# A 1-core transformer block kernel: norm tiles made on VectorE and ScalarE alone, the first two products of a stage run side by side, two waits moved

## What is computed

```python
hl = modulate(rms_norm(xl, norm1_g[i]), mod_l[0], mod_l[1])   # y * (1 + scale) + shift
ol = conv_module(hl, ...)              # block 0: product, gate, 31 taps, layer norm, silu, product
ol, oc = gqa_mixer(hl, hc, ...)        # block 1: qkv product, heads, output product
xl = xl + mod_l[2][:, None, :] * ol
hl = modulate(rms_norm(xl, norm2_g[i]), mod_l[3], mod_l[4])
xl = xl + mod_l[5][:, None, :] * sq_relu_mlp(hl, w_ff1[i], w_ff2[i])
# block 2: rms norm with a gain, an input product, mixers, then experts chosen per token:
# silu(x @ gate) * (x @ up) @ down for each expert slot, gathered and summed
```

## Time and profile before

| | us |
|---|---|
| median of 3 runs | 2501.03 (2499.95 to 2521.93) |
| the profiled execution's own time | 2502.87 |
| its span in the trace | 2501.1 |
| PE busy | 2287.1 |
| DVE busy | 1376.6 |
| ACT busy | 791.2 |
| POOL busy | 733.2 |

### The profile page before, as it was taken

How to read it: one execution, slowest core, us unless ns; L and a number is a source line. 1 busy time by engine, 2 the same in 40 slices (tenths; PEclk the granted TensorE clock), 3 DMA queues, 4 the chain that set the end, 5 groups by cost and what they waited for, 6 DMA issues and landing times.

```text
span 2501.1 us, 30069 instructions
## 1 busy us (share of the span) xinstructions
PE 2287.1 (91%) x11308; PEld 1797.4 (72%) x11308; DVE 1376.6 (55%) x1709; ACT 791.2 (32%) x1068; POOL 733.2 (29%) x409
## 2 busy tenths in 40 slices
PE   6899987899999999897999899999899779799993
PEld 3566746778888888774456688887688667688882
DVE  2488974264444444315663664655222751699994
ACT  2311104221111111331662311211333322577772
POOL 2200001443333333543443544443444034011101
PEclk8899997999999999899999899999899899899996
DMA  8554340162122212130001233333233023499994
GB/s 272 168 167 144 127 165 28 51 252 68 59 67 59 67 59 68 43 91 25 1 1 43 85 93 94 99 92 107 74 93 92 9 71 135 175 397 398 412 397 151
DMA packets 248521, 312.79 MB, mean 125 GB/s; under 512 B 13706, under 2 KB 199787, under 8 KB 236147
## 3 DMA queue, kind: packets, MB, share of 16 engines
q1 hardware_dynamic: 236956, 275.33, 32.6%
q0 software_dynamic: 6688, 25.69, 2.7%
q10 hardware_dynamic: 4791, 10.58, 1.1%
HBM read 286.39 MB, written 25.18 MB: 125 GB/s over the span
## 4 chain that ended last, share of the span: by engine, by line
PE 83%; DVE 8%; DMA 3%; POOL 2%; ACT 2%; issue 2%; DVEq 0%; POOLq 0%; ACTq 0%; SPq 0%
PE acc L494 54%; PE acc L2394 7%; PE pb L2416 4%; PE pb L2046 2%; PE pa L1998 2%; PE acc L2172 2%; DMA mod_raw<-in_w_mod 2%; PE pa L2186 2%; PE pb L2199 2%; PE acc L541 1%; POOL y L620 1%; PE acc L555 1%; DVE hid_hi L1481 1%; PE pa L2384 1%; PE pa L648 1%
## 5 line engine op out<-in xcount | busy, mean ns | idle before, releaser
L477 POOL TENSOR_TENSOR wlo<-raw,whi 128x1024 fp32r<-128x1024 f32 x204 | 509.2, 2496 | 967.3 <-ACT whi L466 967.2
L494 PE MATMUL acc<-ah,whi 128*128 128x256 f32 (+1 forms) x1616 | 514.7, 367 | 57.7 <-DVE al L660 35.7
L466 ACT ACTIVATE whi<-raw 128x1024 fp32r<-128x1024 f32 x218 | 230.4, 1059 | 1054.3 <-PE acc L494 1035.5
L494 PE MATMUL acc<-al,whi 128*128 128x256 f32 (+1 forms) x1616 | 506.9, 363 | 0.0
L494 PE MATMUL acc<-ah,wlo 128*128 128x256 f32 (+1 forms) x1616 | 506.3, 362 | 0.0
L494 PEld LDWEIGHTS acc<-ah,whi 128*128 128x128 f32 x1616 | 307.1, 192 | 119.4 <-issue 42.4
L494 PEld LDWEIGHTS acc<-al,whi 128*128 128x128 f32 x1616 | 310.0, 192 | 47.0 <-issue 0.5
L494 PEld LDWEIGHTS acc<-ah,wlo 128*128 128x128 f32 x1616 | 309.1, 191 | 47.3
L1490 DVE SCALAR_TENSOR_TENSOR x<-acc,mod,x 128x256 f32<-128x256 f32 (+1 forms) x192 | 121.1, 658 | 262.0 <-PE acc L494 261.9
L768 DVE TENSOR_TENSOR expert_lo<-expert_pair,expert_hi 128x1024 fp32r<-128x1024 f32 x192 | 224.4, 1220 | 23.0 <-ACT expert_hi L763 23.0
L494 PE MATMUL acc<-hid_hi,whi 128*128 128x512 f32 (+1 forms) x768 | 230.7, 355 | 0.7 <-DVE x L1490 0.2
(11 more groups left out here) (348 smaller groups left out, 2824.4 us busy)
## 6 DMA issues: line engine op xcount, KB each, us to landing
raw<-in_w_ff SPq DMA_DIRECT2D x128, 512.0 KB, 3.9
mod_raw<-in_w_mod SPq DMA_DIRECT2D x96, 512.0 KB, 5.4
expert_pair<-in_expert_w_gate SPq DMA_DIRECT2D x32, 1024.0 KB, 7.7
expert_pair<-in_expert_w_up SPq DMA_DIRECT2D x32, 1024.0 KB, 7.5
expert_pair<-in_expert_w_down SPq DMA_DIRECT2D x32, 1024.0 KB, 7.2
raw<-in_w_in SPq DMA_DIRECT2D x30, 512.0 KB, 3.9
raw<-in_conv_w_pw SPq DMA_DIRECT2D x24, 512.0 KB, 7.6
expert_rows_dram<-zero_rows POOLq DMA_DIRECT2D x1, 12288.0 KB, 38.4
```

Of the source, the lines that this page charges most:

```text
L466: e.eng.activation(whi[e.n["q"] % 2][:, :], raw[r][:, :], ACT.Copy).then_inc(S["hi_ready"], 1)
L477: e.eng.tensor_tensor(wlo[b][:, :], raw[e.n["g"] % RING][:, :], whi[b][:, :].bitcast(F32), ALU.subtract).then_inc(S["lo_ready"], 1)
L494: ins = e.eng.matmul(o, w, m, start=keys.index(key) == n, stop=len(keys) - 1 - keys[::-1].index(key) == n)
```

## The change

Five edits:

1. A norm tile takes three steps. DVE multiplies x by the root and by the gain or scale in one instruction for each segment, ACT adds the shift and rounds into `ah`, DVE adds the shift and subtracts `ah` into `al`. POOL has no part in it. Tiles run three ahead. The layer norm and the norm with a gain have the same order now.
2. `first_pair`: the first two products behind each of the six norms take turns, tile by tile, in the two PSUM banks. Both need their weights split beforehand, so the second split moves before the tiles on ACT and POOL, and `split_started` is raised one time early in `spread_mean` (in the conv stage by `mod_chunk(18)`), and one time at the last tile of the pair.
3. The first output product behind the attention takes its tiles in the order 0, 1, 2, 3, 4, 6, 5, 7 and waits for `attended` before tile 5.
4. The last expert's down weights go into the buffers 0 to 3.
5. Branches for down pieces that aren't split are dropped (`SPLIT_DOWN` is 4, so they were not used).

```diff
-    def norm_act(e, n, k, segs, k_root, split=True, early=None, affine=None):
+    def norm_act(e, n, k, segs, k_root, early, affine=None):
...
-        if early:
+        early()
+        root(e, k_root, token_stat[:, c0 // P:TOK // P])
+        if n:
             early()
-        root(e, k_root, token_stat[:, c0 // P:TOK // P])
...
         for i in range(KT):
+            e.eng.wait_ge(S["x_scaled"], KT * n + i + 1)
             if affine is None:
...
+                ins = e.eng.activation(ah[:, i, c0:TOK], y[:, i, c0:TOK], ACT.Copy)
             else:
...
-            e.eng.activation(ah[:, i, c0:TOK], y[:, i, c0:TOK], ACT.Copy).then_inc(S["ah_ready"], 1)
-            if k and i == KT - 3:
-                early()
...
+                for s0, s1, v in segs:
+                    at = i + affine[2]
+                    ins = e.eng.activation(ah[:, i, s0:s1], y[:, i, s0:s1], ACT.Identity, bias=mod[:, at:at + 1, v])
+            ins.then_inc(S["ah_ready"], 1)
```

```diff
         def by_root(i):
-            e.eng.tensor_tensor(scaled[i % 3][:, c0:TOK], x[:, i, c0:TOK], token_cols(pa, c0), ALU.mult
-                                ).then_inc(S["x_scaled"], 1)
+            for s0, s1, v in segs:
+                by = cols[:, gain + i:gain + i + 1] if affine is None else msc[:, affine[1], i:i + 1, v]
+                ins = e.eng.scalar_tensor_tensor(out=y[:, i, s0:s1], in0=x[:, i, s0:s1], scalar=by,
+                                                 in1=pa[:, CTX + s0:CTX + s1], op0=ALU.mult, op1=ALU.mult)
+            ins.then_inc(S["x_scaled"], 1)
+
+        def low(i):
+            e.eng.wait_ge(S["ah_ready"], KT * operand + i + 1)
+            for s0, s1, v in segs:
+                hi = ah[:, i, s0:s1].bitcast(F32)
...
+                    ins = e.eng.scalar_tensor_tensor(out=al[:, i, s0:s1], in0=y[:, i, s0:s1], scalar=mod[:, at:at + 1, v],
+                                                     in1=hi, op0=ALU.add, op1=ALU.subtract)
+            ins.then_inc(S["al_ready"], 1)
```

```diff
+    def first_pair(e, segs, operand):
+
+        e.eng.wait_ge(S["lo_ready"], e.at("q", 2))
+        e.eng.wait_ge(S["acc_free"], e.at("u", 2))
+        for t in range(KT):
+            e.eng.wait_ge(S["al_ready"], KT * operand + t + 1)
+            for n in range(2):
+                h, l, bank = whi[(e.n["q"] + n) % 2], wlo[(e.n["q"] + n) % 2], acc[(e.n["u"] + n) % 2]
+                for j, (w, a) in enumerate(((h, ah), (h, al), (l, ah))):
+                    for s0, s1, _ in segs:
+                        ins = e.eng.matmul(bank[:, CTX + s0:CTX + s1], w[:, t * P:t * P + P], a[:, t, s0:s1],
+                                           start=t == 0 and j == 0, stop=t == KT - 1 and j == 2)
+                        if t == KT - 1 and n == 1 and j == 0 and s0 == segs[0][0]:
+                            ins.then_inc(S["split_started"], 1)
+                if t == KT - 1:
+                    ins.then_inc(S["acc_ready"], 1)
+        e.n["u"] += 2
```

```diff
-        load_parts((more, 1), range(8, E_SLOTS, 2))
+        ex = expert_of((more, 1))
+        for s in range(0, 4, 2):
+            sp.wait_ge(S["weights_used"], weights_done((more, 1), s + 1))
+            expert_load(e, ex, s, last=True)
...
-        pe.wait_ge(S["attended"], 1)
-        slots(e, KT, tile(LATENT))
+        pe.wait_ge(S["lo_ready"], e.at("q", 1))
+        pe.wait_ge(S["acc_free"], e.at("u", 1))
+        h, l, bank = whi[e.n["q"] % 2], wlo[e.n["q"] % 2], acc[e.n["u"] % 2]
+        for t in (0, 1, 2, 3, 4, 6, 5, 7):
+            if t == 5:
+                pe.wait_ge(S["attended"], 1)
```

More of the change, by code:

```diff
@@ L478, in split_low, with run_group @@
                             ALU.subtract).then_inc(S["lo_ready"], 1)
-    def run_group(e, group, first=None, last=None, operand=None, per_tile=1):
+    def run_group(e, group, first=None, last=None):
         keys = [g[0] for g in group]
@@ L1390, in _ @@
         e.step(scales(0, 0, 1, V_N1))
-        norm_dve(e, 1, FULL, 1, operand=0, affine=AFFINE[0])
+        norm_dve(e, 0, 1, FULL, 1, 0, AFFINE[0])
         def gated(i):
@@ L1496, in _ @@
         slots(e, KT, to_stream(16, FULL))
-        norm_dve(e, 4, FULL, 3, operand=2, affine=AFFINE[1])
+        norm_dve(e, 1, 4, FULL, 3, 2, AFFINE[1])
         operand_done(e, 3)
@@ L2023, in _, with project, pair @@
         mod_chunk(4, pbk[:, 0:512])
-        def project(i, after=None):
-            product(e, ah, al, FULL, first="split_started" if i % 2 else None, operand=None if i else 0)
+        def project(i):
+            product(e, ah, al, FULL, first="split_started" if i % 2 else None)
             e.n["g"] += 1
             e.n["q"] += 1
+        def pair(segs, operand):
+            first_pair(e, segs, operand)
+            e.n["g"] += 2
+            e.n["q"] += 2
         def turned_at(i, n):
@@ L2106, in down, with up @@
                 product(e, hid_hi[b], hid_lo[b], segs, k=4)
-            feed_forward(e, lambda chunk, j, b: product(
-                e, ah, al, segs, operand=operand if isinstance(chunk, int) and chunk + j == 0 else None), down,
-                beside=beside)
+            def up(chunk, j, b):
+                if isinstance(chunk, int) and chunk == 0 and j < 2:
+                    if j == 0:
+                        first_pair(e, segs, operand)
+                else:
+                    product(e, ah, al, segs)
+            feed_forward(e, up, down, beside=beside)
         spread_mean(e, 1, FULL, 3)
@@ L2122, in sum_heads @@
                           start=n in (0, 1), stop=n in (3, 11)).then_inc(S["qk_summed"], 1)
-        for n in range(12):
+        pair(FULL, 3)
+        sum_heads(0)
+        for n in range(2, 12):
             if n >= 4:
                 pe.wait_ge(S["q_second"], n - 3)
-            product(e, ah, al, LATENT if 2 <= n < 10 else FULL, operand=None if n else 3)
+            product(e, ah, al, LATENT if n < 10 else FULL)
             e.n["g"] += 1
@@ L2253, in used @@
             e.n["q"] += 1
-        for n in range(14):
+        pair(LATENT, 5)
+        for n in range(2, 14):
             if 4 <= n < 8:
@@ L2258, in _ @@
             else:
-                product(e, ah, al, LATENT, operand=None if n else 5)
+                product(e, ah, al, LATENT)
             used()
```

167 lines of the change are left out of this document (60 added, 107 removed).

## The result

| | before | after |
|---|---|---|
| median, us | 2502.35 (4 runs, 2499.95 to 2521.93) | 2476.42 (4 runs, 2473.32 to 2481.44) |
| ratio after / before | | 0.9873, 95% interval 0.984 to 0.9907 |
| span of the profiled execution | 2501.1 | 2474.1 |
| PE busy | 2287.1 | 2284.0 |
| POOL busy | 733.2 | 690.0 |

The forecast was 2468, 32.6 us off the median of before, with a range of 2455 to 2481.

What follows compares the result with a forecast made beforehand. PE, the engine of most of the chain, was taken to lose time waiting, most for `al`, the normed operand's low part. Gains of 39.4 us less 6.8 for clock gave 32.6 off 2501.03: 2468, range 2455 to 2481.

Steps and rivals of the forecast that it cites:

- the forecast case: Whole kernel: all gains arrive, less the clock loss after the third products' waits; 2468, chance 0.62.
- conv: Norm before the conv products: the pair starts without an idle wait and ends at 82.0 instead of 92.1; 10.0 us.
- FF1: Norm before the FF1 products: the third product starts at 519.4 instead of 526.0; 6.6 us.
- head wait: First output product behind the attention: six tiles run first and cover the 3.45 us wait for the last heads; 5.5 us.
- late down weights: Last expert: its down weights load into gate buffers freed earlier, so PE starts at 2453.0, not 2460.39; 7.4 us.
- clock in the third products: After PE's 3 us waits at FF1, conv-out, FF2 and input the clock falls: 1.7 us each, 6.8 lost.
- The tiles: Norm tiles: DVE sets the pace, a pair of instructions every 1.05 us, a tile every 2.10; first tile no earlier.
- The pair: First two products behind a norm, side by side: 16.6 us plus 2.5 for low clock after an idle wait, 19.1.
- The third product: Behind each pair: its weight split may start only at the last tile, so PE idles about 3.0 us.
- That the clock holds: Rival: the clock stays up through the 3 us waits, so the full 39.4 comes off; 2461.6, chance 0.2.
- The partial loss: Rival: conv gains 3 instead of 10 and each third product comes 1 us later; 2480, chance 0.14.
- The slower case: Rival: waiting at every tile keeps PE at the lower clock through all six pairs; 24 us longer, 2525, chance 0.04.

Runs made afterwards that it cites:

- e2: Changed kernel, first product doing its last 3 tiles (5 with one segment) before the second does them, third split starting then; 2462.04, ratio 0.9823.
- e5: The changed kernel itself, unaltered, run again on another chip; 2479.16 against 2513.74 for the kernel before, ratio 0.987.
- e1: Changed kernel with the fourth edit undone: the last expert's down weights go into buffers 8 to 11 again; 2487.59, ratio 0.9913.
- e7: Kernel before with the third and fourth edits alone (output product's tile order, last expert's down buffers); 2501.42, ratio 0.9962.
- e3: Changed kernel with the first product doing its last 2 tiles before the second does them, everywhere; 2478.73, ratio 0.9881.
- lag 1 or 2: Tiles at a pair's end that the first product does before the second: 1 is the changed kernel (2476.42), 2 its variant (2478.73).
- lag 3 and 5: Changed kernel, first product doing its last 3 tiles (two segments) or 5 (one) before the second; 2462.04 without further edits.
- lag 8: Changed kernel with the first product doing all its tiles, then the second; new tile steps and early second splits stay; 2480.86 without further edits.
- e8: e4 with the second split moved back after the sixth tile, the conv stage keeping its early split; 2491.63, ratio 0.993.
- e6: e2 plus junk matmuls while PE waits for a pair's first tile (9 for two segments, 6 for one; not conv); 2459.68, ratio 0.9799.
- e10: e2 plus 8 junk matmuls before two-segment pairs, none for one segment, and scaling two tiles ahead instead of three; 2457.45, ratio 0.9808.
- e4: Changed kernel with one product after the other instead of side by side; new tile steps and early second splits stay; 2480.86, ratio 0.9893.

## Why the prediction was right, step by step

The time lay in the range and the forecast case came true. The terms, as the chain and the timelines of both kernels have them (start of the third product after the spread root, before less after):

| term | predicted | measured |
|---|---|---|
| conv (end of the second product) | 10.0 | 9.9 |
| conv-out | 3.0 | 3.3 |
| FF1 | 6.6 | 6.2 |
| QKV | 3.5 | 3.8 |
| FF2 | 2.7 | 3.5 |
| input | 0.7 | 0.6 |
| head wait | 5.5 | 5.1 |
| late down weights | 7.4 | 7.1 |
| sum | 39.4 | 39.5 |
| clock in the third products | -6.8 | -4.9 |

- **The tiles.** Right: a pair every 1.05, and the first tile no earlier than before (4.45 us after the first scaling, forecast 4.3).
- **The pair.** 19.1 us forecast from its start, 19.3 measured before FF1 (492.14 to 511.4); conv 17.16 against 17.0. For the kernel before, the sum took the third product's start from VectorE's take of the second, or from a row of the chain, which is 0.1 to 0.4 us later than its first matmul, so each norm was forecast that much too high.
- **The third product.** 3.0 us of waiting forecast, 2.69 to 3.19 measured at four norms, for the reason given: e2 takes the cause away and the wait falls to 1.1 and less. The 0.5 us that the prediction took for GpSimd's slow case before FF1 is there (2.88, where a split with VectorE idle takes 2.34).
- **Clock.** The term that was mis-sized: 1.7 at each of four norms, measured 2.9 before FF1, 1.7 before FF2, 0.1 at conv-out and input (fourth less third product in the table above, less the 8.3 or 5.4 of the kernel before). In e5 it was the same, in e1 it was 2.9, 2.8, 1.7 at conv-out and 0.1 at the input product, 7.5 in all. So the term varies from execution to execution, and 6.8 lay within what was seen. The length of the idle wait, from which it was taken, doesn't tell the cases apart: 3.17 us before the input product had no fall, 3.11 before FF2 had one, and 2.7 before conv-out went both ways. What does is open.
- **The rest.** 39.5 - 4.9 = 34.6, and the two profiles lie 27.0 apart. Of the 7.6 us between, 4.1 are the first root. Another 4.3 are a stretch of modulation loads and statistics, from VectorE's last take in the conv module to the layer norm's statistics: 63.3 us before and 67.6 after. What is left over, 0.8 us the other way, is the balance of smaller differences, the largest 1.4 us in the attention.
- **Chance or change.** The first root stood at 57.3 and 60.7 with the old code (before, e7) and between 58.3 and 63.2 in the ten traces with the new; the profile before was the earliest of the twelve. That looks like chance, though a microsecond or two that belong to the new code aren't excluded by so few. The other stretch took 63.3 and 65.9 us with the old code. With the new it took 66.1 to 67.6 in the four traces with lag 1 or 2 (after, e5, e1, e3) and 61.7 to 64.8 in the six with lag 3 and 5 or lag 8, though none of the variants touches its code. As chance this would be odd, but nothing in the runs says what would tie the stretch to the lag, so the cause stays open. Up to 6 us of what a profile with a lag of 3 and 5 has ahead of the kernel after stand here.
- **The size.** The pairing of e5, 34.6 us, is what the sum says, but its own trace has both losses again (first root 59.3, stretch 67.6) and lies 25.2 us under the profile before. So the agreement of 34.6 with 34.6 is luck in part. What the traces show are the terms.
- **The rivals.** That the clock holds: half true (two of four norms in two traces, one of four in e1). The partial loss: its time would have been nearer to the first measurement (2480 against 2476), but not its mechanism; the conv stage kept its whole gain (in e5 3.4 of the 10 us were lost again in the modulation chunk behind it). The slower case, the lower clock through all pairs, did not come: the clock before FF1 is 0.53 up to 497 us and 1.00 from there on. The swinging of the clock between small idles that the Trainium skill (TensorE: Matmul & The Clock Gate, A second HAM failure mode: psum-queue depth-cycling) describes is not in this trace.
- **VectorE beside GpSimd.** The Trainium skill (SBUF — State Buffer, Who interferes with whom) has the one instruction wait for the other's end, a microsecond as the prediction priced it; in this trace the split began 0.1 us after ACT's end, at 511.66, in the middle of VectorE's squaring (511.39 to 512.35), and ran 0.5 longer, with 0.7 of the squaring left. Whether it stood still for that time the trace doesn't tell. Where it cost more was e8: there both engines lost 0.9 to 1.1 us.

## What to carry to other kernels

Two products that share a new operand gain from running side by side only until the operand is complete; from there on run them one after the other, because whatever waits for the first product's buffers (here the next weights' split) can then start while the second product still does its last tiles: 12.7 us in the norms here, beside the 26 to 35 of the whole change. When a helper engine is freed, look at where its remaining work lands: a split beside the engine that sets the pace cost that engine a microsecond here, and a wait of under 2 us that came of it could bring the clock down. And an edit of a few us is read at fixed marks in the trace, relative to the event that starts its stage; between two single profiles the stretches that nobody touched differed by more than most of the edits.

## What the runs showed that was not expected

- The products of FF1 have two speeds at a granted clock of 1.00. From the third to the last take of two-segment products they span 441.0 us in eight of the twelve traces, 449.4 in e1 and e8, 444.4 in e6 and 445.9 in e10. A matmul over 512 columns takes 391 ns on average in e4 and 395 to 403 ns in e8 in the same stretch, with the same instructions in the loop and no wait. The timed runs of e1 fall into two groups some 14 us apart. The 8.4 us of this stretch may be a part of that; the rest, and what sets the speed, were not found.
- VectorE's CAST of one SBUF tile (`hid_hi`) takes 0.56 us by itself and 2.58 beside GpSimd's split of 2.88 (512.38 to 514.96 after; the split ends at 514.54). So one SBUF input is enough for VectorE to be held.
- With 9 junk matmuls in the idle wait of 4.5 us the clock was at 1.00 for the pair behind it: 1.7 to 3.0 us a pair.
- The same norm code had the clock fall before conv-out in one execution (e1) and not in two others (after, e5), after the same wait of 2.7 us.
